# Tanh in place of sigmoid, gate matmuls inside a projection unit, and a row-first out projection in the recurrent stage of a one-core trunk kernel

## The chip, the core and the metric

One core of one Trainium2 chip runs the whole program. The metric is the device time of one execution in microseconds (us): the time before is the median of three runs. The engines are TensorE (PE: matmul; PEld: its weight loads), VectorE (DVE), ScalarE (ACT), GpSimd (POOL) and SyncE (SP), which issues most of the DMAs.

## The reference, cut to what matters

The program computes two layers of a trunk for 256 tokens of width 1024, in float32: a recurrent mixer (RG-LRU), a dense SwiGLU, an attention mixer, and a top-2-of-8 expert SwiGLU. The change touches the recurrent mixer alone.

```python
proj = h @ w_in
y_branch, x_branch = jnp.split(proj, 2, axis=-1)
y_branch = jax.nn.gelu(y_branch)
xc = causal_depthwise_conv(x_branch, conv_w, width 4) + conv_b
r  = jax.nn.sigmoid(einsum('bshi,hij->bshj', xb, w_a) + b_a)      # xb: xc in 8 blocks of 128
gi = jax.nn.sigmoid(einsum('bshi,hij->bshj', xb, w_x) + b_x)
log_a = -LRU_C * r * jax.nn.softplus(-log_lambda)                 # LRU_C = 8
a = jnp.exp(log_a)
b = jnp.sqrt(-jnp.expm1(2.0 * log_a)) * (gi * xc)
_, hseq = lax.associative_scan(_lin_combine, (a, b), axis=1)      # h[t] = a[t] h[t-1] + b[t]
return (hseq * y_branch) @ w_out
```

## The kernel before

**Weights as a stream of units.** Every large matrix is cut into units of 512 rows by 512 columns (1 MB), numbered in the order in which they are used. SP loads unit m into one of 7 `raw` buffers once `lo_done` says that the one 7 units earlier is free. ACT copies it to `whi` (rounded to fp32r, `hi_to`, line 421), DVE writes the rest `raw - whi` to `wlo` (`lo_to`, line 1085), and PE multiplies three times (hi by hi, hi by lo, lo by hi) so that the product has float32 accuracy. `whi` and `wlo` have 3 buffers: ACT may convert unit m when PE has finished unit m-3, which PE counts in `used`. Each engine runs one instruction stream in order, so a call `hi_to(n)` or `lo_to(n)` placed among other work sets the order by hand, and what stands behind it waits with it.

**The recurrent stage.** Units 0 to 3 give the x branch (two halves of 512 channels, `ch` or `g` 0 and 1, two units each), units 4 to 7 the y branch. A unit of these, `weights_unit`, is 48 matmuls of 256 columns, 12 for each of its four channel blocks. ACT copies the x branch to `xpad`, DVE does the convolution into `xc`. After unit 4, PE runs `lru_gates` for both halves (line 741, 16 matmuls in plain float32, two passes each): r into PSUM banks 4 and 5, i into banks 6 and 7; for the second half it waits until ACT has read the first. ACT applies Sigmoid with the bias (line 471), then, once all eight r blocks are there, Exp into `av` (line 477) and Tanh into `rg` (line 478) for each of the eight blocks, then Sqrt on `qf` (line 483), then the gelu of both y halves (line 487). POOL multiplies `gi` by `xc` (line 377). DVE forms `a*a` and `(a*a+1)*tanh` (lines 1192 and 1194), which is `1-a*a`, multiplies by `gi` (1202), scans (1206) and multiplies by the gelu (1209); that is z. ACT rounds z into `hT_hi` (line 492), DVE writes the rest to `hT_lo` (`z_to_lo`, line 1185, which counts `z_lo`).

**The out projection.** Units 8 to 11, `tokens_unit` with 24 matmuls of 512 columns, in the order (column half 0, z half 0), (0, 1), (1, 0), (1, 1). Unit 8 waits for the first half of z, unit 9 for the second. DVE adds columns half 0 to X after unit 9 and half 1 after unit 11 (line 1138). The next norm needs all of X: ACT and DVE sum squares, POOL takes the power, DVE scales, and PE goes on with transposes (line 709).

**The rest** is the dense SwiGLU (to about 345 us), the attention (to about 522 us), the router, and eight blocks of 42 expert units (from about 554 us to the end).

**Table loads.** ACT's functions come in sets, and ACT_TABLE_LOAD rows stand where the set is changed: ahead of Sigmoid, ahead of Exp and Tanh, ahead of Sqrt, ahead of the gelu.

Of the kernel before, what the change touches and what calls it, by code (L numbers as in the profile page):

```python
# [35 lines left out]
LRU_C = 8.0  # L36
# [7 lines left out]
N_IN = 8  # L44
# [11 lines left out]
ALU = mybir.AluOpType  # L56
ACT = mybir.ActivationFunctionType
# [34 lines left out]
def hybrid_trunk(nc, x, norm_mix, norm_ffn, lru_w_in, lru_conv_w, lru_conv_b, lru_w_a, lru_b_a, lru_w_x, lru_b_x,  # L92
                 lru_log_lambda, lru_w_out, fox_w_in, fox_b_f, fox_q_gain, fox_k_gain, fox_w_out, ffn_w_gate,
                 ffn_w_up, ffn_w_down, moe_router, moe_w_gate, moe_w_up, moe_w_down, out):
    with ExitStack() as ctx:
# [3 lines left out]
        def sb(name, shape, dt=F32, where=None):  # L99
            return (where or ctx).enter_context(nc.sbuf_tensor(name, shape, dt))  # L100
# [25 lines left out]
        rms2 = sb("rms2", [P, TT])  # L126
        rstd = sb("rstd", [P, 8])
        mhalf = sb("mhalf", [P, H])
        PAR_CONVW, PAR_CONVB, PAR_BA, PAR_BX, PAR_LAM, PAR_MIX, PAR_FFN = 0, 32, 40, 48, 56, 64, 80
        GAIN = [PAR_MIX, PAR_FFN, PAR_MIX + KT, PAR_FFN + KT]  # L130

# [125 lines left out]
        def front_units():  # L257
            for col in (2, 3, 0, 1):
                for rows in (0, UK):
                    yield lru_w_in[0], rows, col  # L260
            for col in (0, 1):
                for rows in (0, UK):
                    yield lru_w_out[0], rows, col
            yield from swiglu_units(ffn_w_gate[0], ffn_w_up[0], ffn_w_down[0])
            for col in (0, 1, 2, 3, 4, 6, 5, 7):
                for rows in (0, UK):
                    yield fox_w_in[0], rows, col
            for rows in (0, UK):
                for col in (0, 1):
                    yield fox_w_out[0], rows, col  # L270
# [73 lines left out]
        def _(pool):  # L344
# [27 lines left out]
                    pool.dma_start(qkg[half * HD:(half + 1) * HD, i:i + 1], g.rearrange("a d -> d a")  # L372
                                   ).then_inc(small_in, 16)

            for g in range(4):
                pool.wait_ge(sig_i, 2 * g + 2)
                pool.tensor_tensor(gi[:, 2 * g:2 * g + 2], gi[:, 2 * g:2 * g + 2], xc[:, 2 * g:2 * g + 2],
                                   ALU.mult).then_inc(gx_done, 1)
            rms_pow(1)
            rms_pow(2)  # L380
            for cc in range(4):
# [20 lines left out]
        def _(act):  # L402
# [59 lines left out]
                    nc.scalar.activation(xpad[:, 4 * ch + 2 * i:4 * ch + 2 * i + 2, CONV - 1:],  # L462
                                         ps[:, bank].rearrange("p (c t) -> p c t", t=T), ACT.Copy).then_inc(xp_in, 1)

            for ch in range(2):
                hi_to(6 + ch)
                for ready, done, dst, par0, bank0 in ((gate_r, sig_r, rg, PAR_BA, 4), (gate_i, sig_i, gi, PAR_BX, 6)):
                    for i in range(4):
                        c = 4 * ch + i
                        act.wait_ge(ready, 2 * (c // 2) + 2)  # L470
                        nc.scalar.activation(dst[:, c], ps[:, bank0 + i // 2, (i % 2) * T:(i % 2 + 1) * T],
                                             ACT.Sigmoid, bias=par[:, par0 + c:par0 + c + 1]).then_inc(done, 1)

            act.wait_ge(lam_done, 2)
            act.wait_ge(sig_r, KT)
            for c in range(KT):
                nc.scalar.activation(av[:, c], rg[:, c], ACT.Exp, scale=lt[:, 4, c:c + 1]).then_inc(a_exp, 1)
                nc.scalar.activation(rg[:, c], rg[:, c], ACT.Tanh, scale=lt[:, 5, c:c + 1]).then_inc(th_done, 1)
                if c == 3:
                    hi_to(8)  # L480
            for g in range(2):
                act.wait_ge(m2_done, g + 1)
                nc.scalar.activation(qf[:, 4 * g:4 * g + 4], qf[:, 4 * g:4 * g + 4], ACT.Sqrt).then_inc(mult_done, 1)

            for ch in range(2):
                act.wait_ge(used, 2 * ch + 6)
                nc.scalar.activation(yb[:, 4 * ch:4 * ch + 4].rearrange("p c t -> p (c t)"),
                                     ps[:, 2 * ch:2 * ch + 2].rearrange("p b n -> p (b n)"),
                                     ACT.Gelu_apprx_tanh).then_inc(gelu, 1)
            for g in range(2):  # L490
                act.wait_ge(z_done, g + 1)
                nc.scalar.activation(hT_hi[:, 4 * g:4 * g + 4], yb[:, 4 * g:4 * g + 4], ACT.Copy).then_inc(z_hi, 1)
                if g == 0:
                    hi_to(9)
            hi_to(N_FFN)

            act.wait_ge(small_in, 16 * 7)
# [175 lines left out]
        def _(pe):  # L673
# [11 lines left out]
                    if k == UK - 1:  # L685
                        ins.then_inc(used, 1)

            def weights_unit(m, bank, half):

                pe.wait_ge(lo_done, m + 1)  # L690
                for c in range(4):
# [52 lines left out]
            for n in range(8):  # L744
                if n < 2:
                    pe.wait_ge(h_lo, 4 * n + 4)
                if n == 0:
                    pe.wait_ge(par_done, 1)
                weights_unit(n, (4, 6, 0, 2)[n // 2], n % 2)
                if n == 4:  # L750
                    pe.wait_ge(wax_in, 32)
                    pe.wait_ge(xp_in, 4)
                    for ch in range(2):
                        lru_gates(ch)

            for i in range(4):
                if i < 2:
                    pe.wait_ge(z_lo, i + 1)
                tokens_unit(N_IN + i, None, of_hT, UK * (i % 2), TT, lambda t: ps[:, 2 * (i // 2) + t],
                            i % 2 == 0, i % 2 == 1)  # L760


            pe.wait_ge(xn_done, 4)
# [301 lines left out]
        def _(dve):  # L1065
# [69 lines left out]
            def add_to_x(bank, j):  # L1135
# [23 lines left out]
            nc.vector.tensor_scalar(lt[:, 4], lt[:, 1], -LRU_C, None, ALU.mult).then_inc(lam_done, 1)  # L1159
            nc.vector.tensor_scalar(lt[:, 5], lt[:, 1], LRU_C, None, ALU.mult).then_inc(lam_done, 1)  # L1160

            dve.wait_ge(edges, 1)
            for ch in range(2):
                lo_to(2 * ch + 3)
                cs = range(4 * ch, 4 * ch + 4)
                for w in range(CONV):
                    for c in cs:
# [10 lines left out]
                            ins.then_inc(conv_done, 1)  # L1178
                        elif c == cs[-1]:
                            link(ins)  # L1180
            lo_to(7)
            def z_to_lo(g):
                cs = slice(4 * g, 4 * g + 4)
                dve.wait_ge(z_hi, g + 1)
                nc.vector.tensor_tensor(hT_lo[:, cs], yb[:, cs], hT_hi[:, cs].bitcast(F32), ALU.subtract  # L1185
                                        ).then_inc(z_lo, 1)


            for g in range(2):
                q = qf[:, 4 * g:4 * g + 4]  # L1190
                dve.wait_ge(a_exp, 4 * g + 4)
                link(nc.vector.tensor_tensor(q, av[:, 4 * g:4 * g + 4], av[:, 4 * g:4 * g + 4], ALU.mult))
                dve.wait_ge(th_done, 4 * g + 4)
                nc.vector.scalar_tensor_tensor(out=q, in0=q, scalar=1.0, in1=rg[:, 4 * g:4 * g + 4], op0=ALU.add,
                                               op1=ALU.mult).then_inc(m2_done, 1)
                if g == 0:
                    lo_to(8)
            for g in range(2):
                cs = slice(4 * g, 4 * g + 4)
                dve.wait_ge(mult_done, g + 1)  # L1200
                dve.wait_ge(gx_done, 2 * g + 2)
                link(nc.vector.tensor_tensor(gi[:, cs], qf[:, cs], gi[:, cs], ALU.mult))
                if g == 1:
                    z_to_lo(0)
                for c in range(4 * g, 4 * g + 4):
                    ins = nc.vector.tensor_tensor_scan(xc[:, c], av[:, c], gi[:, c], 0.0, ALU.mult, ALU.add)
                link(ins)
                dve.wait_ge(gelu, g + 1)
                nc.vector.tensor_tensor(yb[:, cs], xc[:, cs], yb[:, cs], ALU.mult).then_inc(z_done, 1)
            lo_to(9)  # L1210
            z_to_lo(1)

            dve.wait_ge(consts, 10)
# [3 lines left out]
            dve.wait_ge(small_in, 16 * 7)  # L1217
            nc.vector.tensor_scalar(qkg[:, 0:1], qkg[:, 0:1], float(HD) ** -0.5, None, ALU.mult).then_inc(qkg_done, 1)
            for j in range(2):
                lo_to(N_IN + 2 * j + 3)  # L1220
                dve.wait_ge(used, N_IN + 2 * j + 2)
                add_to_x(2 * j, j)

                if j == 0:

                    dve.wait_ge(small_hi, 2)
                    nc.vector.tensor_tensor(wf2[:, :, H:], wf[:], wf2[:, :, 0:H].bitcast(F32), ALU.subtract
                                            ).then_inc(small_lo, 1)
                    nc.vector.tensor_tensor(rw2[:, :, E:], rw[:], rw2[:, :, 0:E].bitcast(F32), ALU.subtract
                                            ).then_inc(small_lo, 1)  # L1230
# [353 lines left out]
```

## Time and profile before

| what | value |
|---|---|
| median of 3 runs | 1532.16 us (1529.86, 1532.16, 1539.75) |
| the profiled execution, its own time | 1539.95 us |
| its span, first to last instruction | 1538.2 us |
| mean granted TensorE clock | 0.982 |
| TensorE busy | 1504.0 us, 98% of the span |
| VectorE, ScalarE, GpSimd busy | 77%, 63%, 2% |

Times in the rows are microseconds from the start of the span. A timeline row gives the start, the time taken by the group, engine and line, the operation, what it writes and reads, the number of instructions, and in brackets the idle time of the engine before it with what ended it. The granted clock stands as a share of full speed: 1.00 is 2.4 GHz, 0.50 is 1.2 GHz, and a value between is a stretch with both.

### The profile page before, as it was taken

The numbers are of one execution on the slowest core, as the hardware profiler recorded it, in microseconds if no ns is written. First come the engines' busy times: TensorE is split into PE (matmuls) and PEld (weight loads), VectorE is DVE, ScalarE is ACT, GpSimd is POOL, SyncE is SP. The second block draws the span as 40 slices with busy tenths as digits, with TensorE's granted clock in tenths as the row PEclk, the third lists the DMA queues.
The fourth block names the chain that finished last, engine by engine and source line by source line (L and its number), as shares of the span: only waits on it lengthen the run. The fifth ranks groups of instructions, "written<-read, shape, count | busy, mean of one in ns | idle before, by whom it ended". The sixth has DMA issues, their size and how long they took to land.

```text
span 1538.2 us, 20201 instructions
## 1 busy us (share of the span) xinstructions
PE 1504.0 (98%) x7799; PEld 1289.1 (84%) x7799; DVE 1179.6 (77%) x900; ACT 965.0 (63%) x772; POOL 30.4 (2%) x43
## 2 busy tenths in 40 slices
PE   7889999999999899999999999999999999999998
PEld 7879999998788788888888888888888888888887
DVE  7764544456644678889889888888888888988987
ACT  4844433345444557767767767777777776776775
POOL 2100000001100000000000000000000000000000
PEclk9999999999989889999999999999999999999999
DMA  9445555554422559999999999999999999999994
GB/s 339 158 148 182 191 192 183 179 189 135 164 83 82 178 189 378 317 326 360 375 336 358 373 373 331 361 382 314 379 375 324 374 364 336 371 371 329 354 380 164
DMA packets 220011, 434.37 MB, mean 282 GB/s; under 512 B 6960, under 2 KB 9120, under 8 KB 219968
## 3 DMA queue, kind: packets, MB, share of 16 engines
q1 hardware_dynamic: 219504, 433.11, 79.6%
q0 software_dynamic: 368, 0.63, 0.2%
q8 instruction: 30, 0.49, 0.1%
q14 instruction: 13, 0.11, 0.0%
q10 hardware_dynamic: 96, 0.03, 0.0%
HBM read 432.69 MB, written 1.05 MB: 282 GB/s over the span
## 4 chain that ended last, share of the span: by engine, by line
PE 96%; DVE 2%; ACT 1%; issue 0%; DMA 0%; SPq 0%; POOL 0%; DVEq 0%
PE ps L682 25%; PE ps L684 25%; PE ps L683 25%; PE ps L697 4%; PE ps L700 4%; PE ps L699 4%; PE ps L1000 2%; PE ps L1016 2%; PE ps L1009 1%; PE ps L860 0%; PE ps L850 0%; DMA raw<-in_lru_w_in_dram 0%; ACT whi L421 0%; PE ps L978 0%; PE ps L892 0%
## 5 line engine op out<-in xcount | busy, mean ns | idle before, releaser
L1085 DVE TENSOR_TENSOR wlo<-raw,whi 128x2048 fp32r<-128x2048 f32 x408 | 930.8, 2291 | 244.1 <-ACT whi L421 243.3
L421 ACT ACTIVATE whi<-raw 128x2048 fp32r<-128x2048 f32 x408 | 781.6, 1916 | 302.7 <-PE ps L684 223.2
L682 PE MATMUL ps<-whi,hT_hi 128*128 128x512 f32 x1056 | 418.6, 396 | 5.0 <-DVE hT_lo L1185 4.3
L683 PE MATMUL ps<-wlo,hT_hi 128*128 128x512 f32 x1056 | 415.4, 393 | 0.0
L684 PE MATMUL ps<-whi,hT_lo 128*128 128x512 f32 x1056 | 415.2, 393 | 0.0
L682 PEld LDWEIGHTS ps<-whi,hT_hi 128*128 128x128 f32 x1056 | 201.0, 190 | 47.6 <-DVE hT_lo L1185 4.5
L684 PEld LDWEIGHTS ps<-whi,hT_lo 128*128 128x128 f32 x1056 | 200.7, 190 | 42.5
L683 PEld LDWEIGHTS ps<-wlo,hT_hi 128*128 128x128 f32 x1056 | 200.9, 190 | 40.9
L682 PE MATMUL ps<-whi,aT_hi 128*128 128x512 f32 x448 | 179.3, 400 | 0.0
L684 PE MATMUL ps<-whi,aT_lo 128*128 128x512 f32 x448 | 175.3, 391 | 0.0
L683 PE MATMUL ps<-wlo,aT_hi 128*128 128x512 f32 x448 | 174.9, 390 | 0.0
L697 PE MATMUL ps<-hT_hi,whi 128*128 128x256 f32 x576 | 164.6, 286 | 1.2 <-DVE hT_lo L1116 1.2
L700 PE MATMUL ps<-hT_hi,wlo 128*128 128x256 f32 x576 | 164.1, 285 | 0.0
L699 PE MATMUL ps<-hT_lo,whi 128*128 128x256 f32 x576 | 164.1, 285 | 0.0
L697 PEld LDWEIGHTS ps<-hT_hi,whi 128*128 128x128 f32 x576 | 111.6, 194 | 2.2 <-DVE hT_lo L1116 1.9
L699 PEld LDWEIGHTS ps<-hT_lo,whi 128*128 128x128 f32 x576 | 111.6, 194 | 0.2
L700 PEld LDWEIGHTS ps<-hT_hi,wlo 128*128 128x128 f32 x576 | 111.6, 194 | 0.0
L684 PEld LDWEIGHTS ps<-whi,aT_lo 128*128 128x128 f32 x448 | 84.2, 188 | 18.1
L683 PEld LDWEIGHTS ps<-wlo,aT_hi 128*128 128x128 f32 x448 | 84.4, 188 | 16.3
L682 PEld LDWEIGHTS ps<-whi,aT_hi 128*128 128x128 f32 x448 | 84.3, 188 | 15.9
L639 ACT ACTIVATE aT_hi<-ps 128x512 fp32r<-128x512 f32 x56 | 33.5, 599 | 59.1 <-PE ps L1016 59.1
L657 ACT ACTIVATE gt<-ps 128x512 f32<-128x512 f32 x56 | 33.6, 599 | 39.0 <-PE ps L684 38.5
(270 smaller groups left out, 1113.7 us busy)
## 6 DMA issues: line engine op xcount, KB each, us to landing
raw<-in_moe_w_up_dram SPq DMA_DIRECT2D x112, 1024.0 KB, 6.9
raw<-in_moe_w_gate_dram SPq DMA_DIRECT2D x111, 1024.0 KB, 7.0
raw<-in_moe_w_down_dram SPq DMA_DIRECT2D x111, 1024.0 KB, 7.0
raw<-in_fox_w_in_dram SPq DMA_DIRECT2D x16, 1024.0 KB, 5.5
raw<-in_ffn_w_gate_dram SPq DMA_DIRECT2D x14, 1024.0 KB, 5.1
raw<-in_ffn_w_up_dram SPq DMA_DIRECT2D x14, 1024.0 KB, 5.0
raw<-in_ffn_w_down_dram SPq DMA_DIRECT2D x14, 1024.0 KB, 5.0
raw<-in_lru_w_in_dram SPq DMA_DIRECT2D x8, 1024.0 KB, 10.4
```

The lines of the kernel that those rows point to most:

```text
L421: nc.scalar.activation(whi[:, m % HR], src, ACT.Copy).then_inc(hi_done, 1)
L639: nc.scalar.activation(aT_hi[:, c % 2].rearrange("p a s -> p (a s)"), ps[:, 6], ACT.Copy).then_inc(m_thi, 1)
L657: nc.scalar.activation(gt[:, c % 2], ps[:, 4 + c % 2], ACT.Silu).then_inc(m_silu, 1)
L682: mm(dst(t), hi, whi[:, m % HR, k], start=first and k == 0, stop=False)
L683: mm(dst(t), hi, wlo[:, m % HR, k], start=False, stop=False)
L684: ins = mm(dst(t), lo, whi[:, m % HR, k], start=False, stop=last and k == UK - 1)
L697: mm(dst, wh, hT_hi[:, kk], start=half == 0 and k == 0 and c % 2 == 0, stop=False, skip_group_check=True)
L699: mm(dst, wh, hT_lo[:, kk], start=False, stop=False, skip_group_check=True)
L700: ins = mm(dst, wl, hT_hi[:, kk], start=False, stop=half == 1 and k == UK - 1, skip_group_check=True)
L1000: ins = mm(ps[:, 2 + 2 * q + k // 4, (k % 4) * P:(k % 4 + 1) * P], h[:, t, k * P:(k + 1) * P], S[:, t], start=k % 4 == 0 and t == 0, stop= ...
L1016: ins = nc.tensor.transpose(ps[:, 6, a * P:(a + 1) * P], act_s[:, c % 2, a * P:(a + 1) * P], ident[:])
L1085: nc.vector.tensor_tensor(wlo[:, m % HR], src, whi[:, m % HR].bitcast(F32), ALU.subtract).then_inc(lo_done, 1)
```

## The change

The two sigmoids are written with tanh: sigmoid(v) is (1 + tanh(v/2))/2. The halves go into other constants: the bias is halved (`bhalf`, one more DVE operation at the start), the factors `lt[:, 4]` and `lt[:, 5]` are halved and given a second time as bias to Exp and Tanh, `(tanh+1)*xc` is one DVE operation over four blocks where POOL had a multiply over two, and Sqrt gets scale 0.25. ACT's stream is ordered by half: gates and decays of half 0, unit 7, gates and decays of half 1, unit 8. PE runs the gates of half 0 in the middle of unit 4 and those of half 1 after it. The first gelu stands ahead of the first rounding of z, the second behind it and behind unit 9's conversion. On DVE the second part of `lo_to` calls moves earlier: unit 9 is converted before the scans of half 1. The out projection takes both column halves with z half 0 first, in banks 4 to 7, then both with z half 1; the two additions to X follow units 10 and 11.

```diff
@@ front_units
-            for col in (0, 1):
-                for rows in (0, UK):
+            for rows in (0, UK):
+                for col in (0, 1):
                     yield lru_w_out[0], rows, col
@@ pool
-            for g in range(4):
-                pool.wait_ge(sig_i, 2 * g + 2)
-                pool.tensor_tensor(gi[:, 2 * g:2 * g + 2], gi[:, 2 * g:2 * g + 2], xc[:, 2 * g:2 * g + 2],
-                                   ALU.mult).then_inc(gx_done, 1)
@@ act
+            def gates(ch):
+                for ready, done, dst, half, bank0 in ((gate_r, sig_r, rg, 0, 4), (gate_i, sig_i, gi, KT, 6)):
                     for i in range(4):
                         c = 4 * ch + i
                         act.wait_ge(ready, 2 * (c // 2) + 2)
                         nc.scalar.activation(dst[:, c], ps[:, bank0 + i // 2, (i % 2) * T:(i % 2 + 1) * T],
-                                             ACT.Sigmoid, bias=par[:, par0 + c:par0 + c + 1]).then_inc(done, 1)
+                                             ACT.Tanh, scale=0.5, bias=bhalf[:, half + c:half + c + 1]
+                                             ).then_inc(done, 1)
+            def decays(ch):
+                act.wait_ge(sig_r, 4 * ch + 4)
+                for c in range(4 * ch, 4 * ch + 4):
+                    nc.scalar.activation(av[:, c], rg[:, c], ACT.Exp, scale=lt[:, 4, c:c + 1], bias=lt[:, 4, c:c + 1]
+                                         ).then_inc(a_exp, 1)
+                    nc.scalar.activation(rg[:, c], rg[:, c], ACT.Tanh, scale=lt[:, 5, c:c + 1], bias=lt[:, 5, c:c + 1]
+                                         ).then_inc(th_done, 1)
+            def z_to_hi(g):
+                act.wait_ge(z_done, g + 1)
+                act.wait_ge(used, 7 + g)
+                nc.scalar.activation(hT_hi[:, 4 * g:4 * g + 4], yb[:, 4 * g:4 * g + 4], ACT.Copy).then_inc(z_hi, 1)
+            hi_to(6)
             act.wait_ge(lam_done, 2)
-            act.wait_ge(sig_r, KT)
-            for c in range(KT):
-                nc.scalar.activation(av[:, c], rg[:, c], ACT.Exp, scale=lt[:, 4, c:c + 1]).then_inc(a_exp, 1)
-                nc.scalar.activation(rg[:, c], rg[:, c], ACT.Tanh, scale=lt[:, 5, c:c + 1]).then_inc(th_done, 1)
-                if c == 3:
-                    hi_to(8)
+            gates(0)
+            decays(0)
+            hi_to(7)
+            gates(1)
+            decays(1)
+            hi_to(8)
...
-                nc.scalar.activation(qf[:, 4 * g:4 * g + 4], qf[:, 4 * g:4 * g + 4], ACT.Sqrt).then_inc(mult_done, 1)
+                nc.scalar.activation(qf[:, 4 * g:4 * g + 4], qf[:, 4 * g:4 * g + 4], ACT.Sqrt, scale=0.25
+                                     ).then_inc(mult_done, 1)
             for ch in range(2):
+                if ch:
+                    z_to_hi(0)
+                    hi_to(9)
                 act.wait_ge(used, 2 * ch + 6)
...
-            for g in range(2):
-                act.wait_ge(z_done, g + 1)
-                nc.scalar.activation(hT_hi[:, 4 * g:4 * g + 4], yb[:, 4 * g:4 * g + 4], ACT.Copy).then_inc(z_hi, 1)
-                if g == 0:
-                    hi_to(9)
+            z_to_hi(1)
             hi_to(N_FFN)
@@ pe
+                bank = (4, 6, 0, 2)[n // 2]
                 if n == 4:
+                    weights_unit(n, bank, 0, range(0, 2))
                     pe.wait_ge(wax_in, 32)
                     pe.wait_ge(xp_in, 4)
-                    for ch in range(2):
-                        lru_gates(ch)
+                    lru_gates(0)
+                    weights_unit(n, bank, 0, range(2, 4))
+                    lru_gates(1)
+                else:
+                    weights_unit(n, bank, n % 2)
             for i in range(4):
-                if i < 2:
-                    pe.wait_ge(z_lo, i + 1)
-                tokens_unit(N_IN + i, None, of_hT, UK * (i % 2), TT, lambda t: ps[:, 2 * (i // 2) + t],
-                            i % 2 == 0, i % 2 == 1)
+                if i % 2 == 0:
+                    pe.wait_ge(z_lo, i // 2 + 1)
+                tokens_unit(N_IN + i, None, of_hT, UK * (i // 2), TT, lambda t: ps[:, 4 + 2 * (i % 2) + t],
+                            i // 2 == 0, i // 2 == 1)
@@ dve
+            nc.vector.tensor_scalar(bhalf[:], par[:, PAR_BA:PAR_BA + 2 * KT], 0.5, None, ALU.mult)
-            lo_to(7)
+            lo_to(6)
             for g in range(2):
+                dve.wait_ge(sig_i, 4 * g + 4)
+                nc.vector.scalar_tensor_tensor(out=gi[:, 4 * g:4 * g + 4], in0=gi[:, 4 * g:4 * g + 4], scalar=1.0,
+                                               in1=xc[:, 4 * g:4 * g + 4], op0=ALU.add, op1=ALU.mult
+                                               ).then_inc(gx_done, 1)
...
-                if g == 0:
-                    lo_to(8)
+                lo_to(7 + g)
             for g in range(2):
...
                 if g == 1:
                     z_to_lo(0)
+                    lo_to(9)
...
-            lo_to(9)
             z_to_lo(1)
             for j in range(2):
-                lo_to(N_IN + 2 * j + 3)
-                dve.wait_ge(used, N_IN + 2 * j + 2)
-                add_to_x(2 * j, j)
+                lo_to(N_IN + j + 4)
+                dve.wait_ge(used, N_IN + j + 3)
+                add_to_x(4 + 2 * j, j)
```

## Rows read from the trace of the kernel before

**Rows 1.** Section 1 of the page: busy us (share), instructions of each engine.

```profile
PE 1504.0 (98%) x7799; PEld 1289.1 (84%) x7799; DVE 1179.6 (77%) x900; ACT 965.0 (63%) x772; POOL 30.4 (2%) x43
```

**Rows 2.** Waits of the whole span: waiting engine and line, releaser, us, times, longest.

```profile
ACT whi L421 <- PE ps L684: 224.4, 239, 9.3
...
PE ps L682 <- DVE hT_lo L1185: 4.3, 1, 4.3
...
PE ps L850 <- DVE nFT L1317: 2.4, 1, 2.4
```

**Rows 3.** Windows: stretch, busy of PE, PEld, DVE, ACT, POOL, clock, DMA share, GB/s.

```profile
68.00:69.40 1.40, 1.40 (x13) 1.27 (x11) 1.40 (x3) 1.39 (x2) 0.00 (x0) 1.00 0.01 4
74.00:76.00 2.00, 2.00 (x5) 1.62 (x6) 2.00 (x4) 0.23 (x1) 0.00 (x0) 0.50 0.00 0
80.20:98.00 17.80, 17.80 (x80) 14.74 (x79) 11.63 (x12) 6.15 (x6) 0.00 (x0) 1.00 0.71 237
```

**Rows 4.** Timeline of TensorE: start, us, instruction, idle before and its releaser.

```profile
39.38 0.28 PE L697 MATMUL ps<-hT_hi,whi 128*128 128x256 f32 x1
...
45.14 7.07 PE L741 MATMUL ps<-xc,yb 128*128 128x256 f32 x32
51.86 0.47 PE L697 MATMUL ps<-hT_hi,whi 128*128 128x256 f32 x1
...
73.81 0.79 PE L682 MATMUL ps<-whi,hT_hi 128*128 128x512 f32 x1 [4.33 <-DVE hT_lo L1185]
```

**Rows 5.** Timeline of TensorE, the next idle stretch.

```profile
103.85 2.39 PE L709 MATMUL ps<-ident,rows 128*128 128x128 f32 x10 [5.11 <-DVE rows L1110]
```

**Rows 6.** Timeline of ACT, the recurrent stage.

```profile
39.58 1.09 ACT L462 ACTIVATE xpad<-ps 128x512 f32<-128x512 f32 x2 [3.78 <-PE ps L700]
...
46.20 1.70 ACT L471 ACTIVATE rg<-ps,par 128x256 f32<-128x256 f32 x4 [2.44 <-PE ps L741]
...
49.52 1.91 ACT L421 ACTIVATE whi<-raw 128x2048 fp32r<-128x2048 f32 x1
...
54.36 1.28 ACT L477 ACT_TABLE_LOAD   x1
...
65.28 2.02 ACT L483 ACTIVATE xpad<-xpad 128x1024 f32<-128x1024 f32 x2
...
71.37 1.06 ACT L492 ACTIVATE hT_hi<-yb 128x1024 fp32r<-128x1024 f32 x1 [0.82 <-DVE yb L1209]
```

**Rows 7.** Timeline of DVE, end of the recurrent stage.

```profile
46.64 2.28 DVE L1085 TENSOR_TENSOR wlo<-raw,whi 128x2048 fp32r<-128x2048 f32 x1
...
67.64 2.44 DVE L1206 TENSOR_TENSOR_SCAN xc<-av,gi 128x256 f32<-128x256 f32 x4
70.11 1.23 DVE L1209 TENSOR_TENSOR yb<-xc,yb 128x1024 f32<-128x1024 f32 x1
...
72.53 1.23 DVE L1185 TENSOR_TENSOR hT_lo<-yb,hT_hi 128x1024 fp32r<-128x1024 f32 x1
...
98.78 1.22 DVE L1138 TENSOR_TENSOR X<-ps,X 128x1024 f32<-128x1024 f32 x1 [1.14 <-PE ps L684]
```

**Rows 8.** Groups of ACT, us 14 to 110, by form: busy us, mean ns, idle.

```profile
L478 ACT ACTIVATE rg<-rg,lt 128x256 f32<-128x256 f32 x8 | 4.0, 494 | 0.0
L441 ACT ACTIVATE hT_hi<-ps,par 128x256 fp32r<-128x256 f32 x9 | 3.8, 469 | 3.8 <-PE ps L709 3.8
...
L462 ACT ACTIVATE xpad<-ps 128x512 f32<-128x512 f32 x4 | 2.2, 596 | 7.6 <-PE ps L700 7.6
...
L487 ACT ACTIVATE yb<-ps 128x1024 f32<-128x1024 f32 x2 | 1.9, 1022 | 0.0
```

**Rows 9.** Windows of later stretches, columns as in the windows above.

```profile
418.00:427.00 9.00, 9.00 (x27) 6.81 (x27) 4.02 (x3) 2.20 (x12) 0.00 (x0) 0.50 0.02 6
...
433.00:442.00 9.00, 9.00 (x33) 6.88 (x31) 4.11 (x3) 2.82 (x16) 0.00 (x0) 0.62 0.36 117
554.00:1538.00 984.00, 979.72 (x4545) 814.75 (x4543) 865.56 (x525) 711.06 (x470) 0.00 (x0) 1.00 0.96 346
```

More of the change, by code:

```diff
@@ L128, in hybrid_trunk @@
         mhalf = sb("mhalf", [P, H])
+        bhalf = sb("bhalf", [P, 2 * KT])
         PAR_CONVW, PAR_CONVB, PAR_BA, PAR_BX, PAR_LAM, PAR_MIX, PAR_FFN = 0, 32, 40, 48, 56, 64, 80
@@ L463, in _ @@
                                          ps[:, bank].rearrange("p (c t) -> p c t", t=T), ACT.Copy).then_inc(xp_in, 1)
-            for ch in range(2):
-                hi_to(6 + ch)
-                for ready, done, dst, par0, bank0 in ((gate_r, sig_r, rg, PAR_BA, 4), (gate_i, sig_i, gi, PAR_BX, 6)):
+            def gates(ch):
+                for ready, done, dst, half, bank0 in ((gate_r, sig_r, rg, 0, 4), (gate_i, sig_i, gi, KT, 6)):
                     for i in range(4):
@@ L686, in tokens_unit, with weights_unit @@
                         ins.then_inc(used, 1)
-            def weights_unit(m, bank, half):
+            def weights_unit(m, bank, half, columns=range(4)):
                 pe.wait_ge(lo_done, m + 1)
-                for c in range(4):
+                for c in columns:
                     dst = ps[:, bank + c // 2, (c % 2) * T:(c % 2 + 1) * T]
@@ L701, in weights_unit @@
                                  skip_group_check=True)
-                ins.then_inc(used, 1)
+                if c == 3:
+                    ins.then_inc(used, 1)
             def transposes(src, done, banks=(0, 1, 2, 3), k0=0):
@@ L748, in _ @@
                     pe.wait_ge(par_done, 1)
-                weights_unit(n, (4, 6, 0, 2)[n // 2], n % 2)
+                bank = (4, 6, 0, 2)[n // 2]
                 if n == 4:
+                    weights_unit(n, bank, 0, range(0, 2))
                     pe.wait_ge(wax_in, 32)
                     pe.wait_ge(xp_in, 4)
-                    for ch in range(2):
-                        lru_gates(ch)
+                    lru_gates(0)
[3 more added lines that the diff above has]
+                    weights_unit(n, bank, n % 2)
             for i in range(4):
-                if i < 2:
-                    pe.wait_ge(z_lo, i + 1)
-                tokens_unit(N_IN + i, None, of_hT, UK * (i % 2), TT, lambda t: ps[:, 2 * (i // 2) + t],
-                            i % 2 == 0, i % 2 == 1)
+                if i % 2 == 0:
+                    pe.wait_ge(z_lo, i // 2 + 1)
+                tokens_unit(N_IN + i, None, of_hT, UK * (i // 2), TT, lambda t: ps[:, 4 + 2 * (i % 2) + t],
+                            i // 2 == 0, i // 2 == 1)
             pe.wait_ge(xn_done, 4)
@@ L1158, in _ @@
                                                 op1=ALU.add))
-            nc.vector.tensor_scalar(lt[:, 4], lt[:, 1], -LRU_C, None, ALU.mult).then_inc(lam_done, 1)
-            nc.vector.tensor_scalar(lt[:, 5], lt[:, 1], LRU_C, None, ALU.mult).then_inc(lam_done, 1)
+            nc.vector.tensor_scalar(bhalf[:], par[:, PAR_BA:PAR_BA + 2 * KT], 0.5, None, ALU.mult)
+            nc.vector.tensor_scalar(lt[:, 4], lt[:, 1], -0.5 * LRU_C, None, ALU.mult).then_inc(lam_done, 1)
+            nc.vector.tensor_scalar(lt[:, 5], lt[:, 1], 0.5 * LRU_C, None, ALU.mult).then_inc(lam_done, 1)
             dve.wait_ge(edges, 1)
@@ L1200, in _ @@
                 dve.wait_ge(mult_done, g + 1)
-                dve.wait_ge(gx_done, 2 * g + 2)
+                dve.wait_ge(gx_done, g + 1)
                 link(nc.vector.tensor_tensor(gi[:, cs], qf[:, cs], gi[:, cs], ALU.mult))
```

## The prediction

> **What bounds the kernel now.** I read the page's busy line first [rows 1]: TensorE is busy 1504.0 of 1538.2 us, so 34 us are all the idle time there is. The waits of the whole span say what feeds it: the longest of ACT's waits is 224.4 us for PE to free a weight buffer [rows 2], so the copies follow PE and not the reverse, and in the expert part PE is busy 979.72 of 984 us at clock 1.00 [rows 9]. Whatever is won ahead of it shifts the rest, since nothing there goes by an absolute time. Among PE's waits the one in the changed stage is 4.33 us at unit 8, for `hT_lo` of z, once [rows 2, 4]. The windows show what it costs besides: the clock is 1.00 up to 69.4, 0.50 between 74 and 76, and 1.00 again after 80 [rows 3]. The chain into that wait can be followed on ACT and DVE [rows 6, 7]: gates, a table load at 54.36, Exp and Tanh, Sqrt at 65.28, scans, times gelu, and `z_to_lo` at 72.53, which ends at 73.76 just before PE starts.
>
> **What the stretch costs before.** From PE's start at 73.81 to the addition at 98.78 [rows 4, 7] are 24.97 us. At full clock 80 matmuls touch a stretch of 17.80 us [rows 3], 0.2225 each or a little more, since those at its two ends lie partly outside; I take 0.227. Four units of 24 then take 96 x 0.227 = 21.8 us, with about 0.3 us from the last matmul to the add 22.1. The other 2.85 us are the low clock. So idle and clock together are 7.2 us, the most that this edit can win in its own stage.
>
> **The new schedule, step by step.** PE runs unit 4 from 39.38 to 45.14 [rows 4], so its middle is 42.3. All gates take 51.86 - 45.14 = 6.72 us, one half 3.36. New order: half gates 42.3 to 45.6, rest of unit 4 to 48.5, second gates to 51.9. PE does the same work in other order, so unit 7 ends at 73.81 - 4.33 = 69.5 as before, if no wait enters. The two that could: the convolution of half 0 was over long before 46.6, where DVE had finished even half 1 [rows 7], and xpad is complete at 40.7 [rows 6]; the second gates need ACT's read of the first, which I get below as 46.6, 1.9 us ahead.
>
> ACT: a 256-column activation with one operand per partition comes every 0.40 us (four in 1.70 [rows 6], 0.49 each with an overlap of 0.09). The first eight Tanh follow PE and end one pair behind it, 45.6 + 1.0 = 46.6. Then the decays. Here each Exp and Tanh gets a second per-partition operand, which no row shows. The rows without any: 512 columns 596 ns and 1024 columns 1022 ns, a slope of 0.83 ns a column and 383 ns at 256 [rows 8]; with one it is 469, so one costs about 0.09 us. For a second the bounds are 0 and, by the spread that 0.49 on SBUF against 383 allows, 0.2 us (twice what it shows). I take 0.09, the nearest row, so 0.49 an instruction and 3.9 us a half where it was 3.2.
>
> - decays 0: 46.6 + 3.9 = 50.5; unit 7's copy (1.9 [rows 6]): 52.4
> - gates 1: 8 x 0.395 = 3.2: 55.6; decays 1: 59.5; unit 8's copy: 61.4
> - Sqrt: load 1.28 [rows 6], then 1.02 each: 63.7 and 64.7; load and first gelu: 67.0
> - DVE: half 0's `(tanh+1)*xc`, `a*a` and `(a*a+1)*tanh` (3 x 1.24) and unit 7's rest (2.28) lie between 48.9 and 54.9, in ACT's shadow; half 1's end at 61.6, unit 8's rest at 63.9, just as the first Sqrt lands. POOL's work is gone at no gain of its own, as it was never waited for. Then 1.26 + 2.47 (scans) = 67.6, times gelu: 68.8
> - ACT rounds z half 0 (1.06 [rows 6]) to 69.8 while DVE does half 1's multiply to 70.0; `z_to_lo(0)` 1.23: 71.3.
>
> So unit 8 starts at 71.3 in place of 73.81, with a gap of 1.8 us and not 4.33. The term is **-2.5 us**. What is behind it on the queues is late next: ACT's copy of unit 9 ends 71.7, DVE's rest 74.2, scans and product 77.8, rounding 78.9, `z_lo` 2 at 80.2; four small DVE operations (0.6), then unit 10's rest 80.9 to 83.2. PE meanwhile ends unit 8 at 76.8 and unit 9 at 82.2. Both z halves are there, but unit 10's weights are not: it waits 1.0 us, because unit 9's conversion now stands ahead of the scans and unit 10's still behind z. **+1.0 us**. Units 10 and 11 end at 94.1, the last add starts at 94.4 (98.78 before). Unit 13's rest (93.1) is ahead of it by 1.3. The first add comes a unit later, but nothing goes on with half of X here, so it costs nothing. SP's queue gets the same loads with two of the 1 MB units swapped; its waits follow DVE's rests of units 7 to 9 (54.9, 63.9, 74.2 now), for units that PE reads after 100 us, so none is late. The banks 4 to 7 into which the projection now goes were freed by the gates' last read at 55.6.
>
> **The clock.** After a gap of 4.33 it fell; after 5.11 at 103.85 [rows 5] too. With 1.8 us between dense work I take that it holds: **-2.85 us**; if it falls, 0. The start of the stage pays one small DVE operation of 0.17 before unit 3's rest, hidden by DVE's wait for xpad. The Sigmoid load goes (it lay in ACT's wait for the gates), and the one at 54.36 goes as well, if Tanh is in the set that is loaded already: Exp and Tanh alternate behind one load [rows 6, 8], so they share one. Were one load needed at the gates, it would run from 42.5 to 43.8, and cost 0.3.
>
> The sum is -2.5 + 1.0 - 2.85 = -4.35 us, against the profiled 1538.2 us of span (its own run 1539.95). That run lies 7.8 us above the median, all of it outside what is changed, so I put the sum on the median: 1532.16 - 4.4 = **1527.8**. By the bounds of the second operand the last add starts at 93.0 or 96.2, a gain of 5.8 or 2.6: 1526.4 to 1529.6.
>
> The Trainium skill (ScalarE: Activation LUTs, What ACT_TABLE_LOAD costs) says that each per-partition operand adds about 93 ns to an ACTIVATE, which speaks against this change as I price it; the rows show that for the first operand only, and no row has two. The same section gives a switch of set 2.66 us, a load of 1283 ns and a drain of 1380. The trace does not agree: from 54.36 the load takes 1.28 and the next row begins 1.30 after it started. By the page the removed switch would be worth 1.4 us more and the sum would be -5.7; the rows decide.
>
> **The rivals.**
> 1. The clock falls all the same. For it: at 418 to 427 it was 0.50 after a gap of only 2.4 us with short matmuls behind it [rows 2, 9]. Against: dense matmuls stand on both sides here. Then only 1.5 us are won: 1530.7. Chance 0.15.
> 2. Not faster: the low-clock stretches move in the attention's score stage. From 418 to 427 and 433 to 442 the clock is 0.50 and 0.62 while PE is full [rows 9], in all 9 + 6.8 = 16 us at the low level, which cost about 8 us. Its place against the chip's clock control shifts with everything earlier. If it grows from 16 to 25 us, 4.4 us are given back: 1532.2, and with more, slower (18 us more: 1536.8). For it: three runs of one program lie 9.9 us apart. Chance 0.17, the other side of zero beyond 9 us more.
> 3. The same mechanism, or free second operands, in its favour: 1526.4 less 4 us of low clock, 1522. Chance 0.13.
> 4. The change does not do what it says: ACT's stream, with unit 7's copy between the halves, is late by a further 2.5 us (a set reload inside the decays would do it), and the gap stays at 4.3. Two loads of 1.28 give it. Against: one load serves sixteen alternating calls. The add would start at 99.8, +1: 1533.2. Chance 0.05.
>
> My forecast has 0.50. For 8 in 10 the range runs from rival 3 at 1521.5 to the reach of rival 2 at 1534.5. What a measurement of this kernel can tell from no change is about 1%, 15 us; all my cases lie within it. For faster by over 1% (under 1516.8) I leave 0.03, for slower by over 1% 0.02, within 1% 0.95.
>
> **What the profile after would show.** PE's wait before unit 8 of 1 to 2.5 us, the clock at 1.00 from 69 to 98; no table load between 20 and 60 us; decays at 0.58 us each, starting every 0.49 (at 0.40 each, the gain is 1.4 greater); a second wait of about 1 us before unit 10; the last add near 94.4. I am wrong if the wait before unit 8 stays over 3.5 us, if the clock is 0.50 after it, or if the stretch from 100 to 550 us changes by more than 3 us, in which case the total says little about the edit.

## The result, and the profile after

The changed kernel takes 1542.99 us (median of 20 runs) beside 1535.16 us for the kernel before (20 runs, among them those shown above); the ratio is 1.0055, with a 95% interval of 1.0041 to 1.007. So it is slower by about 8 us, where 1527.8 us and a gain of 4.4 were forecast. One of the 20 runs after (2165.08 us, at a mean clock of 0.649) and one of e10's ten below (3032.53 us) were slow ones and are left out of the ratios. The profiled execution after has a span of 1539.4 us.

The stage that was changed did become faster. TensorE's waits in it, timeline of the changed kernel (columns as in [rows 4]; line 692 is what line 682 was):

```profile
69.21 0.50 PE L692 MATMUL ps<-whi,hT_hi 128*128 128x512 f32 x1 [1.49 <-DVE hT_lo L1202]
...
80.93 0.47 PE L692 MATMUL ps<-whi,hT_hi 128*128 128x512 f32 x1 [0.54 <-DVE wlo L1100]
...
97.17 3.25 PE L720 MATMUL ps<-ident,rows 128*128 128x128 f32 x14 [5.11 <-DVE rows L1125]
```

The wait of 4.33 us before unit 8 [rows 4] is 1.49, and a new one of 0.54 stands before unit 10. The windows of the same stretch show that the clock held, where it had fallen to 0.50 [rows 3]:

```profile
69.00:71.00 2.00, 1.79 (x8) 1.49 (x9) 1.50 (x2) 1.54 (x2) 0.00 (x0) 1.00 0.00 0
71.00:75.00 4.00, 4.00 (x19) 3.31 (x18) 3.96 (x6) 0.00 (x0) 0.00 (x0) 1.00 0.45 127
75.00:81.00 6.00, 5.46 (x25) 4.23 (x23) 4.79 (x8) 5.18 (x4) 0.00 (x0) 1.00 0.24 93
81.00:92.00 11.00, 11.00 (x48) 8.83 (x48) 8.04 (x6) 3.66 (x4) 0.00 (x0) 1.00 0.82 286
```

ACT's timeline begins with the second copy to `xpad`, a place that both kernels reach with the same work behind them; then an activation with two per-partition operands follows every 0.49 us, and the first table load after it is Sqrt's:

```profile
37.84 1.09 ACT L459 ACTIVATE xpad<-ps 128x512 f32<-128x512 f32 x2 [3.78 <-PE ps L710]
...
44.90 0.60 ACT L474 ACTIVATE av<-rg,lt 128x256 f32<-128x256 f32 x1
45.39 0.60 ACT L476 ACTIVATE rg<-rg,lt 128x256 f32<-128x256 f32 x1
...
57.44 1.93 ACT L418 ACTIVATE whi<-raw 128x2048 fp32r<-128x2048 f32 x1
59.39 1.28 ACT L494 ACT_TABLE_LOAD   x1
```

The groups of ACT by form give the durations, 604 ns with two such operands and 478 with one:

```profile
L476 ACT ACTIVATE rg<-rg,lt 128x256 f32<-128x256 f32 x8 | 4.8, 604 | 0.0
L467 ACT ACTIVATE gi<-ps,bhalf 128x256 f32<-128x256 f32 x8 | 3.2, 478 | 0.0
```

On DVE's timeline the additions to X follow:

```profile
86.65 1.23 DVE L1153 TENSOR_TENSOR X<-ps,X 128x1024 f32<-128x1024 f32 x1 [1.47 <-PE ps L694]
...
92.09 1.23 DVE L1153 TENSOR_TENSOR X<-ps,X 128x1024 f32<-128x1024 f32 x1 [1.14 <-PE ps L694]
```

From that copy to the last add the stage took 98.78 - 39.58 = 59.20 us before [rows 6, 7] and takes 92.09 - 37.84 = **54.25 us** now: 4.95 us are won. (The copy itself comes 1.7 us earlier. That is no work of the change: it stands at 37.8 to 38.1 us also in e2, e5, e10, e13, e14 and e15 below, whose program up to that copy is that of the kernel before, and at 39.5 to 40.0 in the other variants of that kernel.)

How much the low clock costs in this stage differs between executions. In those kernels below that leave its instructions and the places of `whi`, `wlo` and `hT` as before, it takes from 57.82 us (e9) to 59.20 (before). The wait for the first half of z is 4.3 to 4.4 us alike. In the kernel before the clock is 0.50 for the 6 us after PE's start at 73.81; in e13 (57.88 us in all) PE starts at 72.06, and the windows show the clock back at 1.00 by 76:

```profile
74.00:76.00 2.00, 2.00 (x8) 1.64 (x7) 1.97 (x3) 0.35 (x1) 0.00 (x0) 0.75 0.00 0
76.00:78.00 2.00, 2.00 (x10) 1.65 (x10) 2.00 (x2) 2.00 (x2) 0.00 (x0) 1.00 0.00 0
```

So 4.95 us is the gain over the profiled execution of before, and 3.6 the gain over the shortest of these.

Then the gain goes. DVE's additions to X mark the stages; in the expert part there is one group of four at each block, and last the one at the end. Before:

```profile
675.47 2.72 DVE L1512 SCALAR_TENSOR_TENSOR X<-ps,ccol,X 128x512 f32<-128x512 f32 x4
...
798.78 2.72 DVE L1512 SCALAR_TENSOR_TENSOR X<-ps,ccol,X 128x512 f32<-128x512 f32 x4
```

```profile
1532.90 2.78 DVE L1512 SCALAR_TENSOR_TENSOR X<-ps,ccol,X 128x512 f32<-128x512 f32 x4
```

After:

```profile
670.07 2.72 DVE L1532 SCALAR_TENSOR_TENSOR X<-ps,ccol,X 128x512 f32<-128x512 f32 x4
...
794.30 2.72 DVE L1532 SCALAR_TENSOR_TENSOR X<-ps,ccol,X 128x512 f32<-128x512 f32 x4
```

```profile
1534.08 2.79 DVE L1532 SCALAR_TENSOR_TENSOR X<-ps,ccol,X 128x512 f32<-128x512 f32 x4
```

| from mark to mark | before | after | re-aligned (e1) | before + 64 bytes (e2) |
|---|---|---|---|---|
| second xpad copy to last add of the mixer | 59.20 | 54.25 | 54.30 | 58.90 |
| to last add of the dense SwiGLU | 246.75 | 249.54 | 246.88 | 248.75 |
| to last add of the attention | 177.68 | 178.43 | 180.74 | 173.63 |
| to the adds at 675.47 (router, first block) | 152.26 | 150.01 | 150.66 | 151.57 |
| seven blocks, to the last adds | 857.43 | 864.01 | 857.43 | 864.01 |

A block takes 124.23 us where it took 123.31 (by turns 123.31 and 123.27), and the change has not an instruction there. The clock is 1.00 from 554 us to the end in both. The groups by form, us 700 to 1500, show which matmuls it is (columns as in [rows 8]); before, then after:

```profile
L683 PE MATMUL ps<-wlo,hT_hi 128*128 128x512 f32 x731 | 284.8, 390 | 0.0
...
L683 PE MATMUL ps<-wlo,aT_hi 128*128 128x512 f32 x364 | 142.1, 390 | 0.0
```

```profile
L693 PE MATMUL ps<-wlo,hT_hi 128*128 128x512 f32 x726 | 282.7, 389 | 0.0
...
L693 PE MATMUL ps<-wlo,aT_hi 128*128 128x512 f32 x360 | 142.4, 396 | 0.0
```

Those with `hT` as stationary operand take 390 and 389 ns, those with `aT` 390 and 396. `aT`, `fT` and `qT` are allocated behind `mhalf`, and the change puts a tile there: `bhalf`, 64 bytes on each partition. `hT`, `whi` and `wlo` stand ahead of it. By the order and sizes of the program's tiles, whi starts at byte 73856, hT_hi at 143488, aT_hi at 207744 before and 207808 after: 128, 128, 128 and 192 modulo 256 (the remainder after division by 256).

### The profile page after: what moved, and what is told of

It reads as the page before. It is cut to its first block, busy times and chain, and to the rows that moved or that the text cites. A ratio compares the mean times of both kernels' runs of the same rounds, so it can differ in the third digit from the quotient of the medians.

```text
span 1539.4 us, 20200 instructions
## 1 busy us (share of the span) xinstructions
PE 1507.5 (98%) x7799; PEld 1283.1 (83%) x7799; DVE 1181.9 (77%) x903; ACT 963.4 (63%) x770; POOL 25.4 (2%) x39
## 4 chain that ended last, share of the span: by engine, by line
PE 96%; DVE 2%; ACT 1%; issue 0%; DMA 0%; SPq 0%; POOL 0%; DVEq 0%; ACTq 0%
PE ps L692 25%; PE ps L694 24%; PE ps L693 24%; PE ps L707 5%; PE ps L710 5%; PE ps L709 4%; PE ps L1015 2%; PE ps L1031 2%; PE ps L1024 1%; PE ps L752 0%; PE ps L875 0%; PE ps L865 0%; ACT whi L418 0%; DMA raw<-in_lru_w_in_dram 0%; PE ps L907 0%
## 5 line engine op out<-in xcount | busy, mean ns | idle before, releaser
L667 ACT ACTIVATE gt<-ps 128x512 f32<-128x512 f32 x56 | 33.6, 600 | 38.8 <-PE ps L694 37.8
```

What stands on the lines that cost most here:

```text
L667: nc.scalar.activation(gt[:, c % 2], ps[:, 4 + c % 2], ACT.Silu).then_inc(m_silu, 1)
```

## The experiments

Each kernel was timed against the kernel before on the same chip. Theory A at first: the stationary operand's start against multiples of 128 bytes.

**e1: the change, with bhalf at the end**

```diff
-        bhalf = sb("bhalf", [P, 2 * KT])
...
             lt = sb("lt", [P, 6, 8], where=a1)
+            bhalf = sb("bhalf", [P, 2 * KT], where=a1)
```

> The changed kernel with one edit: the new tile bhalf (64 bytes a partition) is the last tile of the recurrent stage and no longer stands ahead of some fifty others, so every other tile has the address it had before the change. Theory A (a stationary operand that starts 64 bytes off a multiple of 128 costs TensorE about 6 ns a matmul): the down-projection matmuls of the experts go back from 0.2338 to 0.2275 us, an expert block from 124.23 to 123.29 us, the dense SwiGLU from 249.5 to about 247; in all 10 us less than the changed kernel and about 5 us less than the kernel before: ratio 0.9967. Theory B (the new order or the new instructions slow the later stages): nothing changes, ratio 1.0055. Theory C (only the clock's chance): ratio anywhere, the pitch of the expert matmuls unchanged at 0.2338.

Measured: 1528.78 us, ratio 0.997 (0.9954 to 0.9985): faster than the kernel before and, by the ratios, than the changed one. DVE's adds in the expert part stand again 123.31 us apart:

```profile
670.46 2.72 DVE L1532 SCALAR_TENSOR_TENSOR X<-ps,ccol,X 128x512 f32<-128x512 f32 x4
...
793.77 2.72 DVE L1532 SCALAR_TENSOR_TENSOR X<-ps,ccol,X 128x512 f32<-128x512 f32 x4
```

The stage itself is unchanged at 54.30 us. So the order and the instructions of the change cost nothing later; where its tile stands does.

**e2: the kernel before with 64 unused bytes**

```diff
         mhalf = sb("mhalf", [P, H])
+        sb("filler", [P, 16])
```

> The kernel before with an unused tile of 64 bytes a partition where the change puts bhalf; nothing else. Theory A: 1344 expert matmuls with aT, 336 with fT and 96 with qT as stationary operand get 6 ns dearer, 10 us in all: ratio 1.0066, an expert block 124.23 us. Theory B: ratio 1.000, a block 123.29 us.

Measured: ratio 1.006 (1.0037 to 1.0083), a block 124.24 us (adds at 670.97 and 795.21), seven blocks 864.01 us, the same as in the changed kernel to the last digit.

```profile
670.97 2.72 DVE L1513 SCALAR_TENSOR_TENSOR X<-ps,ccol,X 128x512 f32<-128x512 f32 x4
...
795.21 2.72 DVE L1513 SCALAR_TENSOR_TENSOR X<-ps,ccol,X 128x512 f32<-128x512 f32 x4
```

A tile that nothing reads or writes makes the kernel before as slow as the change did.

**e3: with 128 bytes** (the filler with 32 columns)

> As the run with 64 bytes, but with an unused tile of 128 bytes, so that all later tiles move and keep their place against multiples of 128. Theory A: no difference from before, a block 123.29 us. If any move at all costs (the distance between tiles, the end of the memory): as with 64 bytes, 124.23 us.

Measured: ratio 1.0069 (1.0042 to 1.0095).

```profile
671.08 2.72 DVE L1513 SCALAR_TENSOR_TENSOR X<-ps,ccol,X 128x512 f32<-128x512 f32 x4
...
795.44 2.72 DVE L1513 SCALAR_TENSOR_TENSOR X<-ps,ccol,X 128x512 f32<-128x512 f32 x4
```

A block of 124.36 us: theory A's rule of 128 falls here, though it had the operand and the price for 64 bytes right.

**e4: 64 bytes ahead of aT_hi alone**, and 64 behind aT_lo

> The kernel before with 64 unused bytes ahead of aT_hi and 64 behind aT_lo: these two tiles alone start 64 bytes off a multiple of 128. Theory A: the matmuls with aT as stationary operand take 0.2335 us, those with fT and qT 0.227 as before; a block 124.23 us, 8 blocks 7.5 us, ratio 1.0049. Were it fT, the router's tiles or the vector engines' operands that cost: 123.29 us and ratio 1.000.

Measured: ratio 1.0053 (1.0032 to 1.0074), a block 124.20 us, the dense SwiGLU 246.72. It is this operand, and the other tiles that e2 moved do not matter to the block.

**e5, e6: fT by 32 and aT by 256, then the mirror**

> The kernel before with fT_hi and fT_lo 32 bytes further and aT_hi and aT_lo 256 bytes further (unused tiles ahead of them). A shift by 64 and one by 128 both cost, so the rule of 128 has fallen. Theory A1 (good places repeat every 256 bytes): an expert block 123.3 us as before, the matmuls with fT dearer, the dense SwiGLU from the last add of the mixer to its own last add 248.7 and not 246.75 us. Theory A2 (only the very place of before is good, by its distance to another tile): block 124.2 us too.

> The kernel before with fT 256 bytes further and aT 32 bytes further: the mirror of the last run. A1: dense SwiGLU 246.75 us, a block dearer (124.2 us, or less if 32 bytes cost less than 64). A2: both dearer.

Measured: e5 ratio 1.0005 (0.9985 to 1.0025), a block 123.27 us, the SwiGLU 248.70. e6 ratio 1.0035 (1.0011 to 1.0058), a block 124.23, the SwiGLU 247.36, 0.6 more than the 246.75 expected. For aT, 256 bytes cost nothing, so the good places repeat (A1); for fT 0.6 us is left, which no row explains.

**e7, e8: what the place is measured against**

```diff
+        sb("fill_w", [P, 32])
         whi = sb("whi", [P, HR, UK, CW], F32R)
         wlo = sb("wlo", [P, HR, UK, CW], F32R)
+        sb("fill_v", [P, 32])        # e7 only
```

> The kernel before with whi and wlo, the moving operands, 128 bytes further (0 and not 128 modulo 256), all else at its old place modulo 256. Theory R (what counts is the place of the stationary against the moving operand modulo 256): all matmuls that stream whi or wlo get dearer, also those with hT: 126 units of 42 x 3 matmuls in 8 blocks, (2688 + 1344 + 336 + 480 + 96) x 6 ns = 30 us, ratio 1.019, a block 123.3 + 504 x 0.006 = 126.3 us. Theory S (the stationary operand's own place modulo 256 counts): no change, ratio 1.000, block 123.3 us.

> The kernel before with every tile from whi on 128 bytes further, so that moving and stationary operands keep their distances and all stand at 0 modulo 256. Theory R: no change, ratio 1.000, block 123.3 us. Theory S: stationary tiles stand at 0 modulo 256, hT among them, so every matmul of 512 columns is 6 ns dearer: block 126.3 us, ratio 1.019.

Measured: e7 1559.43 us, ratio 1.0164 (1.0131 to 1.0197); e8 ratio 0.9992 (0.9972 to 1.0011). Groups by form of e7 in the same stretch:

```profile
L685 PE MATMUL ps<-wlo,hT_hi 128*128 128x512 f32 x711 | 280.5, 395 | 0.0
...
L685 PE MATMUL ps<-wlo,aT_hi 128*128 128x512 f32 x360 | 141.8, 394 | 0.0
```

Adds of e7, then of e8:

```profile
681.30 2.72 DVE L1514 SCALAR_TENSOR_TENSOR X<-ps,ccol,X 128x512 f32<-128x512 f32 x4
...
807.16 2.72 DVE L1514 SCALAR_TENSOR_TENSOR X<-ps,ccol,X 128x512 f32<-128x512 f32 x4
```

```profile
675.34 2.72 DVE L1513 SCALAR_TENSOR_TENSOR X<-ps,ccol,X 128x512 f32<-128x512 f32 x4
...
798.60 2.72 DVE L1513 SCALAR_TENSOR_TENSOR X<-ps,ccol,X 128x512 f32<-128x512 f32 x4
```

With the moving operand alone at another place, now the `hT` matmuls are slow too (395 ns) and a block takes 125.86 us (2.55 over 504 matmuls, 5.1 ns each; 126.3 had been expected). With both moved together it takes 123.26. What counts is the distance between stationary and moving operand modulo 256 bytes (theory R); the place of the stationary one by itself (S) is ruled out by both runs. ACT and DVE write whi and wlo too, and e7 moved them against `raw`, from which they are made; e8 did the same and cost nothing, so that is not the cause.

**e9, e13, e14, e15: the rest of the circle**

> The kernel before with fT 96 and aT 192 bytes further than their old places, whi and wlo unmoved: the last two distances of the scan. Theory R (any distance between the stationary and the moving operand that is no multiple of 256 bytes costs): an expert block 124.2 us, the dense SwiGLU 248.7 us. Were it graded, the cost would be below that of a distance of 128.

> The kernel before, aT 224 and fT 160 bytes further. If the cost falls evenly from 128 towards 256 (192 gave 1.7 ns a matmul, 128 gave 6.4): a block of 123.3 to 123.4 us for 224. If 0 is a single good place in a field of costs near 6 ns and 192 was a second one: 124.2 us. If the best place lies between 192 and 256: below 123.2 us.

> The kernel before, aT 160 and fT 224 bytes further. Even fall: 160 between 128 (124.36 us) and 192 (123.57 us), about 124.0 us a block. Single good places: 124.2 us or more.

> The kernel before, aT 96 and fT 192 bytes further. With 64 at 124.23 and 128 at 124.36 us: 124.2 to 124.4 us a block, whatever the rule on the other side. The dense SwiGLU with fT at 192: 336 x 1.7 ns = 0.6 us over 246.75, so 247.3 us, where 64 gave 248.75.

Ratios: 1.0028, 1.0033, 1.006, 1.0063. By the adds, with the block's excess over 123.31 divided by its 168 matmuls with aT:

| aT further by (bytes) | 0 | 32 | 64 | 96 | 128 | 160 | 192 | 224 | 256 |
|---|---|---|---|---|---|---|---|---|---|
| a block, us | 123.31 | 124.23 | 124.20 | 124.45 | 124.36 | 124.31 | 123.57 | 124.07 | 123.27 |
| ns a matmul | 0 | 5.5 | 5.3 | 6.8 | 6.3 | 6.0 | 1.5 | 4.5 | 0 |
| the dense SwiGLU, us, with fT further by as much | 246.75 | 248.70 | 248.75 | 249.64 | 248.45 | 249.25 | 247.89 | 249.44 | 247.36 |

Successive blocks of one run differ by up to 0.08 us, so a figure of the third row is good to about half a nanosecond. The last row has each fT distance from the run in which fT stood there, a second reading of the same effect: 192 costs less than the rest, which cost 1.7 to 2.9 us over 336 matmuls. It is coarser, as the 0.6 us left at 256 show.

My expectation that any distance costs the same (e9) missed at 192, and the even fall (e13) missed at 224, which is dearer than 192. Of the SwiGLU, 248.7 was expected in e9 and 247.3 in e15; they took 249.64 and 247.89. None of these steps of 32 bytes is better than 0, so the kernel before leaves no time there; the changed kernel does.

**e10: the order of the out projection alone**, in the kernel before

> The kernel before with the out projection alone in the new order (units, banks, additions), no new tile. Measured from the second copy to xpad to the last add to X: 59.20 us before, 54.25 after the change. By the steps of the prediction the first z half is no earlier and unit 9 had no wait to lose: 59.2 us, ratio 1.000. Rival: the order is what the stage gained by, 54 to 55 us, ratio 0.997.

Measured: ratio 0.9998 (0.9973 to 1.0022). Adds:

```profile
91.75 1.22 DVE L1138 TENSOR_TENSOR X<-ps,X 128x1024 f32<-128x1024 f32 x1 [1.14 <-PE ps L684]
...
97.19 1.23 DVE L1138 TENSOR_TENSOR X<-ps,X 128x1024 f32<-128x1024 f32 x1 [1.14 <-PE ps L684]
```

The xpad copy is at 38.05, so the stage takes 59.14 us, and the wait before unit 8 is still 4.38. Alone, the order shows no gain.

**e11: e1 with the old order** (units, banks, additions of the kernel before)

> The re-aligned changed kernel with the out projection in the old order. Unit 8 starts as in the changed kernel, but unit 9 needs the second z half, which comes 3.3 us after unit 8 ends; the wait of 0.5 us for unit 10 goes. Theory: 54.25 + 2.8 = 57.0 us from the second xpad copy to the last add, or up to 59.9 if the clock falls after that wait. Rival (the order is worth nothing in either kernel): 54.3 us.

Measured: ratio 1.0016 (0.9995 to 1.0037); copy at 37.81, last add at 96.11: 58.30 us. TensorE's waits:

```profile
69.19 0.50 PE L692 MATMUL ps<-whi,hT_hi 128*128 128x512 f32 x1 [1.48 <-DVE hT_lo L1202]
...
77.93 0.80 PE L692 MATMUL ps<-whi,hT_hi 128*128 128x512 f32 x1 [3.01 <-DVE hT_lo L1202]
```

The wait for the second half of z has 3.01 us, and after it the clock falls for a part:

```profile
78.00:82.00 4.00, 4.00 (x11) 3.19 (x12) 3.91 (x6) 2.22 (x2) 0.00 (x0) 0.60 0.09 12
82.00:84.00 2.00, 2.00 (x11) 1.65 (x10) 0.95 (x1) 0.00 (x0) 0.00 (x0) 1.00 0.92 282
```

**e12: e1 with Sigmoid**, full biases and one operand in Exp and Tanh

> The re-aligned changed kernel with Sigmoid kept (full bias, no second operand in Exp and Tanh, no factor in Sqrt; gi times xc is the same DVE operation with a 0 in place of the 1). ACT must now change its set before each of the two decays and before the second gates: 3 x 1.28 us, less 16 x 0.09 for the second operands: z half 0 comes 2.4 us later, 56.7 us from the second xpad copy to the last add, with a wait of 3.9 us before unit 8; if the clock falls then, 59.5. Rival (tanh is worth nothing, the new order alone gains): 54.3 us.

Measured: ratio 0.999 (0.9971 to 1.0008); copy at 37.99, last add at 97.69: 59.70 us, with a wait before unit 8 of 5.26 and the clock at 0.50 behind it. ACT's timeline:

```profile
41.77 1.28 ACT L467 ACT_TABLE_LOAD   x1 [0.90 <-PE ps L752]
...
46.12 1.28 ACT L474 ACT_TABLE_LOAD   x1
...
52.54 1.28 ACT L467 ACT_TABLE_LOAD   x1
...
56.88 1.28 ACT L474 ACT_TABLE_LOAD   x1
```

z is later than in e1 by 5.26 - 1.49 = 3.8 us and not by 2.4: a fourth load, at 41.77, stands behind ACT's wait for the first gates (0.90) and is not hidden; 4 x 1.28 - 16 x 0.09 = 3.7. In the kernel before, the load ahead of the first Sigmoid stood before the wait (42.48, with 2.44 us idle after it). The prediction priced a load at the gates by that row, at 0.3 us, and the expectation above leaves it out; in e12 it costs its 1.28.

## Why the prediction was wrong

**The step that failed**, for most of the miss, is the cost of the new tile. The prediction counts `bhalf` as "one small DVE operation of 0.17", and it says of all that lies behind the stage that "whatever is won ahead of it shifts the rest". A tile is also an address. Its 64 bytes changed the distance of fT, qT and aT to the weights that TensorE streams against them: 1344 matmuls with aT, 336 with fT and 96 with qT at 5.3 to 6 ns make about 10 us. e2 measures it alone: 0.6% of 1535 is 9.2 us (0.37 to 0.83%, 5.7 to 12.7 us), and in its rows seven blocks take 6.58 us more and the SwiGLU 2.00. That term was missing from the sum; e1 takes it out again.

**A second, smaller part is low clock elsewhere.** The tile and the gain of e1 do not add up to the result: -0.3% and +0.6% make +0.3%, and 0.55% was measured. Each run has its span and its mean granted clock on record. Their product is an estimate of what the span would be at full clock throughout, and the rest of the span is what the low clock cost. Means over the runs:

| | runs | span x clock, us | rest, us |
|---|---|---|---|
| before (timed beside e1 and e2) | 23 | 1509.4 | 23.3 |
| e1 | 12 | 1507.2 | 20.6 |
| e2 | 6 | 1519.1 | 21.6 |
| the changed kernel | 19 | 1516.8 | 24.3 |

The sum closes in the column of span x clock. e1 is 2.2 below before, and its waits in the stage are 2.84 - 0.54 = 2.3 us shorter; e2 is 9.7 above; the changed kernel is 7.4 above, which is 9.7 - 2.3. The last column says that e1 spends 2.7 us less on the low clock than before, about what the stage won (2.85), and that the changed kernel does not: it spends 24.3 us where 23.3 - 2.85 = 20.5 were to be. These 3.8 us are of the kind of rival 2. The rest goes from 18 to 29 us between single runs of the changed kernel (clock 0.988 to 0.981), so the difference of its mean to that of e1 is uncertain by about 1 us. Why the changed kernel has it and e1 has not is open. Together, -4.35 as forecast, -0.8 for waits in the stage shorter than forecast, +9.7 for the tile and +3.8 for the clock make +8.35 us; the means of the runs lie 8.4 apart (1534.4 and 1542.8).

**The rest of the sum held.** Without the tile's displacement (e1) the change is worth a ratio of 0.997, 4.6 us (2.3 to 7.1), where -4.35 was summed:

- The gap before unit 8 was to be 1.8 us and is 1.49 (term -2.5, measured -2.84). ACT's steps, less the 1.7 us by which this execution is earlier: end of decays 0 forecast at 48.8 and measured at 48.84, of the second gates 53.9 and 53.5, unit 8's copy forecast to start at 57.8 and starting at 57.44.
- The second operand adds 604 - 494 = 110 ns to an activation's duration and 0.09 us to the spacing, as taken, so the free second operands of rival 3 are out. Here the Trainium skill (ScalarE: Activation LUTs, What ACT_TABLE_LOAD costs), with 93 ns for each, agrees with the spacing. Its 2.66 us for a change of set does not agree with these rows: loads in e12 are followed by the next activation 1.28 to 1.30 us later, and the sum in e12 comes out with 1.28.
- The second wait, for unit 10's weights, was to be 1.0 us and is 0.54.
- The clock held at 1.00 after a wait of 1.49 us: the 2.85 us of the profiled execution are won in the stage, though that is the upper end of what the low clock costs there (57.82 to 59.20 us above). After 3.01 us (e11) and 5.26 (e12) it fell. Rival 1 is out.
- Exp and Tanh gates need no load: none stands between 20 and 59 us. Rival 4 is out, and e12 shows what loads there would have cost: with four of them the stage is back at 59.7.
- The order was costed by me as part of the whole. e10 and e11 show how it works: no gain alone, 4.0 us (58.30 - 54.30) together with the earlier first half of z, since only then is the second half what PE waits for. I had not asked what each part is worth without the other.

**Rival 2** had the right sign, and for the larger part a wrong reason. The stretches of low clock in the attention do move (177.68, 178.43, 180.74 and 173.63 us in the table), but between single executions of kernels that are faster and slower alike; by the table of clocks it made 3.8 us, and the 9.7 of the tile sit in the SwiGLU and the blocks, at clock 1.00. One sign of being wrong came true, that the stretch from 100 to 550 us changes by more than 3: from the mixer's last add to the attention's it grew from 424.43 to 427.97 us. I had meant it as a sign of the clock, which says little about the edit; 2.79 of these 3.54 us are the SwiGLU, where the tile had moved fT. The tile's cost was to be seen ahead only by asking what the new tile moves, and the trace of before has no row with another distance, so its price was not to be had from it.

**What stays open.** Why the distance costs, and why 192 bytes cost only a quarter to a third of the others, was not found. Nor was it found where the changed kernel spends its 3.8 us more of low clock, and what qT costs by itself: its 96 matmuls lie in the attention, whose length moves by more than that with the clock. The ratios have intervals of 2 to 5 us to either side, so what is smaller rests on the rows alone.

## What to carry to other kernels

A tile that is added has an address, and so have all those behind it: put new tiles last, or compare the start of each stationary tile with its moving one modulo 256 bytes before and after (shown here for fp32r matmuls of 512 columns alone). When a change is slower than its own stage shows, compare the duration of one instruction form, and the time of one repeated block, in stages that were not touched. A reordering is worth what the next late thing allows. Here the new order of the out projection gave nothing without the earlier z (59.14 us), the earlier z little without that order (58.30), and both together 54.30.

## What the runs showed of the hardware that I had not expected

A matmul of 512 columns of fp32r with a 128 by 128 stationary tile is issued about every 0.227 us when the two operands' start addresses are equal modulo 256 bytes, and takes 1.5 to 6.8 ns more at the other distances tried. Moving both by 128 bytes changed nothing (e8), moving either alone did (e4, e7). The matmuls of 256 columns, where the weights are stationary and hT moves, took 283 ns in e7 and 284 before: no cost was seen there. The Trainium skill (TensorE: Matmul & The Clock Gate, Step-by-step: what each phase is for) says that loading the next tile's weights does not take SBUF read bandwidth from the running matmul. If the two reads were independent, their distance could not matter; in these runs it does, by up to 3%, and the measurement decides, though what they share was not shown.
